# HGRN scores in a hybrid backbone step: who sums the masked levels

## The chip, the core and the metric

The kernel is one program on one core of a Trainium2 chip. The metric is the device time of one execution, in microseconds (us). The engines of the core work side by side, each on its own queue in strict order, and meet only at semaphores: TensorE (PE: matmuls into PSUM; PEld: its weight loads), VectorE (DVE), ScalarE (ACT), GpSimd (POOL) and SyncE (SP, here only issuing DMAs).

## The reference, cut to what matters

Two layers run over 640 tokens (512 latent, 128 context). Each layer has a projection, windowed attention, a gated DeltaNet, HGRN2, an output projection and an FFN (SwiGLU in layer 0, experts in layer 1). The change is in HGRN2. Per direction and head, over chunks of tokens:

```python
b = jnp.cumsum(lf, axis=2)
dec = masked_exp(tri, b[:, :, :, None, :] - b[:, :, None, :, :])
A = jnp.einsum('bhik,bhjk,bhijk->bhij', qc, kc, dec)
o = jnp.einsum('bhik,bhkv->bhiv', qc * jnp.exp(b), S) + A @ vc
S = S * jnp.exp(bl)[..., None] + jnp.einsum('bhck,bhcv->bhkv', kc * jnp.exp(bl[:, :, None] - b), vc)
```

`A` is the matrix of scores: it is zero where the key lies behind the query, and the decay between key and query differs in every one of the 64 channels, so it is no plain matmul.

## The kernel before

The kernel works in chunks of 128 tokens, five per layer (n = 0 to 4, the last one is the context), both directions and four heads at once. A chunk is cut into four **units** x = 0 to 3 (direction and pair of heads); unit u = 4n + x, so 20 units in a layer, and this stage takes about 100 us in each of the two layers.

The decay is split by **levels**: at each of seven powers of two, pairs of blocks share a midpoint, and the decay from key to query is a product of one factor for each side. A matmul of the weighed keys with the weighed queries gives the scores of a level, and a mask keeps the entries that belong to it. Levels that reach no further than 32 tokens, and the diagonal, are the six **near** ones: they are computed as blocks of 32 x 32, masked, and summed. The wider levels need no mask and are copied.

Per unit, with the names of the code:
- `exponents(u)` (PE): four f16 matmuls of 512 columns into slot 0 of PSUM. `decays(u)` (ACT, L1304, L1305) takes the exponential and frees the slot.
- `weigh(u)` (DVE): two products of 128 x 896, the weighed queries and the weighed keys.
- scores (PE, job `A{u}`, slots 2 and 3): 48 small near matmuls and six wide ones. They wait for `weigh(u)`.
- mask (DVE, L2093): 128 x 384 out of PSUM, times `near`, into the buffer `AC[n % 2]`, which holds six levels of 8 x 32 columns. It frees the slot of the scores.
- `wide(u)` (ACT, L1362): three copies of the wide blocks, after the mask.

Per chunk:
- `collect(n)` (DVE, L2055): after the mask of x = 3, three additions (768, 256 and 256 columns) sum the six levels of `AC`.
- `place(n)` (ACT, L1370): four copies of 32 x 256 put the sum on the diagonal blocks of `AH`. It runs on ACT in unit 4(n+1), after `decays(u + 2)`.
- `keys(n + 1)`: PE turns the next chunk's keys and sums its log gates into slot 1 (job `hk`, L2669) in unit 4n; ACT copies them out.
- `carry(n)` (PE, in unit 4(n+1) + 1): the output of the chunk and the update of the state, from `AH`.
- `upper_gates(n + 2)` (ACT, L1278 and L1281): four steps in unit 4n + 2, for n < 3 only.

What sets the order: each engine's list is written out by hand, and `psum_plan` gives each PSUM job one of four slots and a turn in it. `open_(job)` on PE waits until the job before it in the same slot has been freed. PE's order in one unit is exponents(u + 2), scores of u, then for x = 0 `keys(n + 1)`, for x = 1 `carry(n - 1)`. ACT's order is decays(u + 2), for x = 0 `place(n - 1)` and `keys(n + 1)`, `wide(u)`, then for x = 2 `upper_gates(n + 2)`. DVE's is weigh(u + 1), for x = 2 the update of the state, the mask of u, and for x = 3 `collect(n)`. Behind the last unit, PE sums squares (job `rsL`) and starts the output projection (`mixer`), which waits for weights that ACT and POOL (L804) split in two.

Of the kernel before, what the change touches and what calls it, by code (L numbers as in the profile page):

```python
# [15 lines left out]
ALU = mybir.AluOpType  # L16
ACT = mybir.ActivationFunctionType
# [135 lines left out]
def psum_plan():  # L153
# [4 lines left out]
    for l in range(DEPTH):  # L158
# [27 lines left out]
        for u in range(UNITS):  # L186
            n, x = divmod(u, 4)
            j += [f"{2 + u % 2}:A{u}"]
            j += [f"0:E{u + 2}"] if u + 2 < UNITS else []
            j += [f"1:hk{n + 1}"] if x == 0 and n < 4 else []  # L190
            j += [f"1:rs{x - 1}"] if u in (1, 2) else []
            j += [f"1:hs{n - 1}"] if x == 1 and n else []
        j += ["1:rsL", "0:wo0", "1:hs4", "2:wo1", "1:rsC", "3:wo2", "1:wo3", "0:wo4", "2:wo5", "1:wo6", "0:wo7"]
# [70 lines left out]
def backbone_kernel(nc, x_prompt, x_sample, cache_k, cache_v, state_gdn, state_hgrn, c, c_ctx, w_mod, b_mod, w_in,  # L264
# [12 lines left out]
    with ctx:  # L277
# [160 lines left out]
        def mixed(i, k):  # L438
# [56 lines left out]
            "hg_ready lp_hi lp_lo kk_exp kk_ready kw_ready qb_ready qe_ready ke_ready ac_ready ah_ready o_zero o_sq oc_ready oc_sq rs_ready o_ready "  # L495
# [519 lines left out]
        def _(act):  # L1015
# [66 lines left out]
            for l in range(DEPTH):  # L1082
# [282 lines left out]
                def place(n):  # L1365

                    L.need("ac_ready")
                    for b in range(4):
                        r = slice(32 * b, 32 * b + 32)
                        L.do(a.activation(AH[n % 2][r, :, r], AC[n % 2][r, 0], ACT.Copy), "ah_ready" if b == 3 else None)  # L1370
# [286 lines left out]
        def _(dve):  # L1657
# [3 lines left out]
            def tt(o, x, y, op, to=None, job=None):  # L1661
                ins = v_.tensor_tensor(o, x, y, op)  # L1662
                L.free(ins, job) if job else L.do(ins, to)
# [118 lines left out]
            for l in range(DEPTH):  # L1782
# [272 lines left out]
                def collect(n):  # L2055

                    A = AC[n % 2]
                    tt(A[:, 0:3], A[:, 0:3], A[:, 3:6], ALU.add)
                    tt(A[:, 0], A[:, 0], A[:, 1], ALU.add)
                    tt(A[:, 0], A[:, 0], A[:, 2], ALU.add, to="ac_ready")  # L2060

# [12 lines left out]
                for u in range(UNITS):  # L2074
# [14 lines left out]
                    if x == 0 and n >= 2:  # L2089
                        L.need("ah_ready")  # L2090
# [5 lines left out]
                    if x == 3:  # L2096
                        collect(n)
# [5 lines left out]
                L.need("ah_ready", 2)  # L2103
# [144 lines left out]
        def _(pe):  # L2248
# [107 lines left out]
            for l in range(DEPTH):  # L2356
# [381 lines left out]

                def carry(n):

                    L.need("ah_ready")
# [23 lines left out]
                for u in range(UNITS):  # L2765
# [25 lines left out]
                    close(ins, J(f"A{u}"))  # L2791
                    if x == 0 and n < 4:
                        keys(n + 1)
# [7 lines left out]

                L.need("o_sq")
# [265 lines left out]
```

## Time and profile before

| | us |
|---|---|
| median of 3 runs | 2450.79 (2449.39 to 2457.24) |
| the profiled execution | 2452.5 |
| its span, first to last instruction | 2450.7 |
| PE busy | 2143.4 (87%) |
| DVE busy | 1462.0 (60%) |
| ACT busy | 1284.6 (52%) |
| POOL busy | 750.9 (31%) |
| PE's granted clock, mean | 0.94 of full |

The stage of the change lies at about 518 to 622 us (layer 0) and 1591 to 1695 us (layer 1). Busy shares over the whole span say little about it. A matmul's end is modelled and overlaps the next one's start, so how long TensorE holds its queue is better read from the starts of its rows. A granted clock of 1.00 is 2.4 GHz, 0.50 is 1.2 GHz.

### The profile page before, as it was taken

To read this page: it belongs to the slowest core of one execution; us is meant where nothing else is said; L and a number is where in the kernel's file an instruction comes from. 1 tells how busy PE (TensorE), PEld (TensorE's weight loads), DVE (VectorE), ACT (ScalarE), POOL (GpSimd) and SP (SyncE) were. 2 spreads that over 40 slices of the span, in tenths; PEclk is the share of its full clock that TensorE was granted. 3 is DMA by queue.
4 is the path that set the end of the run, shared out by engine and by line. 5 is a ranking of instruction groups with operands and counts; after the bars stand their busy time and mean duration, and the time that the engine had idled before them with its cause. 6 is when DMAs were issued, how large, how long until landed. Compare 5 with 4: busy or idle time off the path is not lost.

```text
span 2450.7 us, 54596 instructions
## 1 busy us (share of the span) xinstructions
PE 2143.4 (87%) x23078; PEld 1334.2 (54%) x23078; DVE 1462.0 (60%) x1822; ACT 1284.6 (52%) x1664; POOL 750.9 (31%) x557
## 2 busy tenths in 40 slices
PE   5998987878989999999898878888969999999990
PEld 3765656755565555555765557654644444444440
DVE  2256735559362121215567665386379999999976
ACT  3443753456534242423533654465268877887862
POOL 0422115332314242423232234333122333333321
PEclk8999987998999999999999888898979999999995
DMA  9222990020212222316220000020276677990023
GB/s 276 98 88 73 309 293 11 3 56 4 72 52 86 69 88 66 103 51 176 81 93 24 1 10 3 3 57 22 92 255 212 224 269 277 329 317 35 27 104 137
DMA packets 215385, 278.46 MB, mean 114 GB/s; under 512 B 28177, under 2 KB 188797, under 8 KB 215039
## 3 DMA queue, kind: packets, MB, share of 16 engines
q1 hardware_dynamic: 203776, 243.60, 30.9%
q0 software_dynamic: 8432, 29.89, 3.3%
q8 instruction: 166, 2.72, 0.5%
q10 hardware_dynamic: 2959, 1.83, 0.3%
q14 instruction: 52, 0.43, 0.1%
HBM read 368.35 MB, written 29.11 MB: 162 GB/s over the span
## 4 chain that ended last, share of the span: by engine, by line
PE 52%; issue 16%; DVE 14%; POOL 8%; ACT 7%; DMA 3%; SPq 1%; POOLq 0%; DVEq 0%; ACTq 0%
PE ps L2268 49%; POOL mix L968 5%; DVE arena L1662 2%; DMA wbuf<-in_w_mod 1%; DVE mix L1670 1%; DVE mix L1662 1%; PE ps L2475 1%; ACT arena L1142 1%; DVE mix L1666 1%; DVE const L1662 1%; DVE yg L1662 1%; DVE hT L1662 1%; DVE xT L1662 1%; POOL mix L971 1%; DVE arena L1666 1%
## 5 line engine op out<-in xcount | busy, mean ns | idle before, releaser
L2268 PE MATMUL ps<-hT,mix 128*128 128x512 f16 (+2 forms) x3024 | 380.0, 288 | 25.1 <-DVE hT L1662 15.2
L2268 PE MATMUL ps<-w,xgT 128*128 128x512 f16 x1632 | 365.4, 381 | 7.3 <-DVE w L2163 7.3
L2268 PEld LDWEIGHTS ps<-hT,mix 128*128 128x128 f16 x3024 | 230.0, 99 | 172.8 <-issue 19.5
L2163 DVE SCALAR_TENSOR_TENSOR w<-wst,w 128x2048 f16<-128x2048 f32 x136 | 310.0, 2320 | 22.7 <-ACT w L1523 22.7
L1000 POOL TENSOR_TENSOR a<-aval,a 128x256 f16<-128x256 f32 x68 | 159.0, 2338 | 371.1 <-ACT a L1571 371.1
L2268 PEld LDWEIGHTS ps<-w,xgT 128*128 128x128 f16 x1632 | 157.4, 98 | 186.0 <-issue 10.5
L1523 ACT ACTIVATE w<-wst 128x2048 f16<-128x2048 f32 x136 | 251.5, 1899 | 6.4 <-DMA xs_rows<-htok,slot_i 6.4
L2268 PE MATMUL ps<-mix 128*128 128x512 f16 (+5 forms) x1856 | 203.5, 286 | 14.5 <-POOL mix L971 8.8
L2268 PE MATMUL ps<-hT,arena 128*128 128x128 f16 (+1 forms) x1440 | 201.2, 301 | 1.1 <-DVE const L1662 1.1
L2268 PE MATMUL ps<-w2m,aT 128*128 128x512 f16 x816 | 188.7, 381 | 5.5 <-DVE aT L2201 5.5
L2268 PEld LDWEIGHTS ps<-mix 128*128 128x128 f16 (+3 forms) x1856 | 120.3, 122 | 88.4 <-POOL mix L971 12.4
L2169 DVE SCALAR_TENSOR_TENSOR w2m<-wst,w2m 128x2048 f16<-128x2048 f32 x68 | 155.8, 2292 | 15.6 <-ACT w2m L1531 15.1
L2127 DVE SCALAR_TENSOR_TENSOR mix<-ps,mix 128x640 f32<-128x640 f32 x22 | 18.1, 825 | 239.3 <-PE ps L2268 239.3
L2268 PEld LDWEIGHTS ps<-hT,arena 128*128 128x128 f16 x1440 | 112.0, 99 | 87.7 <-issue 5.4
L804 POOL TENSOR_TENSOR arena<-wbuf,arena 128x2048 f16<-128x2048 f32 x24 | 100.0, 4165 | 190.7 <-ACT arena L1031 190.6
L968 POOL TENSOR_TENSOR mix<-wbuf,mix 128x2048 f16<-128x2048 f32 x33 | 134.2, 4081 | 57.0 <-ACT mix L1475 57.0
L2268 PEld LDWEIGHTS ps<-w2m,aT 128*128 128x128 f16 x816 | 79.9, 98 | 103.0 <-DVE aT L2201 6.3
L2268 PE MATMUL ps<-arena 64*32 64x32 f32 (+5 forms) x4320 | 103.8, 218 | 31.7 <-issue 17.9
L1531 ACT ACTIVATE w2m<-wst 128x2048 f16<-128x2048 f32 x68 | 129.4, 1903 | 0.2 <-PE ps L2268 0.2
L971 POOL TENSOR_TENSOR mix<-mix 128x640 f16<-128x640 f32 x22 | 30.7, 1395 | 258.2 <-ACT mix L1484 258.2
L2134 DVE TENSOR_TENSOR arena<-arena,ps 128x640 f32<-128x640 f32 x80 | 65.6, 821 | 73.7 <-PE ps L2268 73.7
L2268 PEld LDWEIGHTS ps<-arena 64*32 64x32 f32 (+3 forms) x4320 | 69.9, 115 | 64.2 <-issue 40.5
(360 smaller groups left out, 3604.5 us busy)
## 6 DMA issues: line engine op xcount, KB each, us to landing
wst<-in_moe_w SPq DMA_DIRECT2D x204, 1024.0 KB
wbuf<-in_w_mod SPq DMA_DIRECT2D x40, 1024.0 KB
wbuf<-in_ffn_w SPq DMA_DIRECT2D x33, 1024.0 KB
wbuf<-in_w_in SPq DMA_DIRECT2D x20, 1024.0 KB
xs_rows<-in_table SPq DMA_DIRECT2D x17, 512.0 KB, 6.3
ys_rows<-yb POOLq DMA_DIRECT2D x17, 512.0 KB, 4.0
wbuf<-in_w_out SPq DMA_DIRECT2D x32, 256.0 KB
xg<-xs_rows POOLq DMA_DIRECT2D x16, 512.0 KB, 5.6
```

Of the source, the lines that this page charges most:

```text
L804: L.do(g.tensor_tensor(split_parts(what)[1], wpiece(WP[f"{l}.{what}"][0], n), split_parts(what)[0], ALU.subtract), "w_lo")
L968: g.tensor_tensor(v[1], wpiece(j), v[0], ALU.subtract).then_inc(sg["w_lo"], 1)
L971: g.tensor_tensor(a2[1][:, t], gbuf[:, t], a2[0][:, t], ALU.subtract).then_inc(sg["a_lo"], 1)
L1000: g.tensor_tensor(a16[:, s % 2, 1, :], aval[:, s % 2, :], a16[:, s % 2, 0, :], ALU.subtract).then_inc(sg["m_alo"], 1)
L1523: a.activation(quarter(s, p)[0], staged(s, p), ACT.Copy, scale=WS).then_inc(sg["m_hi13"], 1)
L1531: a.activation(w2p[s % 2][0], staged(s, 2), ACT.Copy, scale=WS).then_inc(sg["m_hi2"], 1)
L1662: ins = v_.tensor_tensor(o, x, y, op)
L1666: ins = v_.tensor_scalar(o, x, s1, s2, op0, op1)
L2134: v_.tensor_tensor(yacc[:, m], yacc[:, m], ps[:, b, 0:NT], ALU.add).then_inc(ps_free[b], 1)
L2163: v_.scalar_tensor_tensor(out=q[1], in0=staged(s, p), scalar=WS, in1=q[0], op0=ALU.mult, op1=ALU.subtract).then_inc(sg["m_lo13"], 1)
L2169: v_.scalar_tensor_tensor(out=q[1], in0=staged(s, 2), scalar=WS, in1=q[0], op0=ALU.mult, op1=ALU.subtract).then_inc(sg["m_lo2"], 1)
L2268: return mm_(o, w, x, start=first, stop=last, skip_group_check=True)
```

## The change

VectorE's three additions per chunk go. In their place PE multiplies each of the six masked levels by the identity matrix and lets PSUM add them up: six f32 products of 128 x 256 in a new job `ac{n}`. ACT's `place` reads the sum from PSUM instead of from `AC`. For n = 0 to 3 the job is put in PE's list right behind the scores of unit 4(n + 1) and ahead of `keys`; for n = 4 it stands behind the last unit, ahead of `rsL`. It takes slot 1 of PSUM, between the jobs that already use that slot: in units 4, 8 and 12 the next job there is `hk` of `keys`. The semaphores `ac_ready` and `ah_ready` go; the slot's own take their place. `AC` is written again only after the job has been filled two chunks before.

```diff
             j += [f"0:E{u + 2}"] if u + 2 < UNITS else []
+            j += [f"1:ac{n - 1}"] if x == 0 and n else []
             j += [f"1:hk{n + 1}"] if x == 0 and n < 4 else []
...
-        j += ["1:rsL", "0:wo0", "1:hs4", "2:wo1", "1:rsC", "3:wo2", "1:wo3", "0:wo4", "2:wo5", "1:wo6", "0:wo7"]
+        j += ["1:ac4", "1:rsL", "0:wo0", "1:hs4", "2:wo1", "1:rsC", "3:wo2", "1:wo3", "0:wo4", "2:wo5", "1:wo6", "0:wo7"]
...
                 def place(n):
 
-                    L.need("ac_ready")
+                    s = L.full(J(f"ac{n}"))[:, 0:256].rearrange("p (m i) -> p m i", m=8)
                     for b in range(4):
                         r = slice(32 * b, 32 * b + 32)
-                        L.do(a.activation(AH[n % 2][r, :, r], AC[n % 2][r, 0], ACT.Copy), "ah_ready" if b == 3 else None)
+                        ins = a.activation(AH[n % 2][r, :, r], s[r], ACT.Copy)
+                        if b < 3:
+                            L.do(ins)
+                    L.free(ins, J(f"ac{n}"))
...
-                def collect(n):
-
-                    A = AC[n % 2]
-                    tt(A[:, 0:3], A[:, 0:3], A[:, 3:6], ALU.add)
-                    tt(A[:, 0], A[:, 0], A[:, 1], ALU.add)
-                    tt(A[:, 0], A[:, 0], A[:, 2], ALU.add, to="ac_ready")
-
...
                     if x == 0 and n >= 2:
-                        L.need("ah_ready")
+                        L.full(J(f"ac{n - 2}"))
...
-                    if x == 3:
-                        collect(n)
...
-                L.need("ah_ready", 2)
                 update(SH, L.full(J("hs4")), ebl[1], J("hs4"), 4, 6)
...
+                def collect(n):
+
+                    L.done(J(f"A{4 * n + 3}"))
+                    s = open_(J(f"ac{n}"))
+                    for v in range(6):
+                        ins = mm(s[:, 0:256], ident, AC[n % 2][:, v].rearrange("p m i -> p (m i)"), v == 0, v == 5)
+                    close(ins, J(f"ac{n}"))
+
                 def carry(n):
 
-                    L.need("ah_ready")
+                    L.done(J(f"ac{n}"))
...
                     close(ins, J(f"A{u}"))
+                    if x == 0 and n:
+                        collect(n - 1)
                     if x == 0 and n < 4:
                         keys(n + 1)
...
+                collect(4)
                 L.need("o_sq")
                 s = open_(J("rsL"))
```

## Rows read from the trace of the kernel before

**Rows 1.** Windows: chunks 1 to 4, then 1 to 3: length; busy PE, PEld, DVE, ACT, POOL; PEclk.
```profile
545.25:565.97 20.72, 15.72 (x508) 9.75 (x505) 19.23 (x26) 15.13 (x35) 5.13 (x8) 0.87 0.01 3
565.97:584.08 18.11, 16.11 (x504) 10.32 (x505) 16.67 (x21) 12.09 (x31) 6.18 (x8) 0.86 0.02 5
584.08:599.89 15.81, 15.39 (x504) 10.08 (x505) 15.23 (x18) 10.41 (x26) 5.75 (x7) 0.89 0.01 3
599.89:615.61 15.72, 11.56 (x489) 8.05 (x490) 11.93 (x18) 8.66 (x21) 3.90 (x4) 0.99 0.02 4
1617.72:1638.72 21.00, 14.37 (x505) 9.34 (x505) 19.70 (x25) 15.12 (x35) 6.18 (x8) 1.00 0.01 4
1638.72:1657.11 18.39, 15.72 (x504) 10.23 (x505) 16.38 (x21) 12.10 (x31) 5.54 (x8) 0.89 0.02 4
1657.11:1673.53 16.42, 15.23 (x504) 9.75 (x505) 15.21 (x18) 10.41 (x26) 6.11 (x7) 0.92 0.02 4
```
**Rows 2.** Chain of waits through layer 1's chunks: start, us, what, instructions.
```profile
1634.19 0.57 DVE mix L1662
...
1638.72 3.08 PE ps L2268 x90
1641.80 1.04 PE ps L2669 x4
...
1644.62 7.16 PE ps L2268 x186
...
1652.59 0.57 DVE mix L1662
...
1657.11 3.43 PE ps L2268 x90
...
1674.24 0.97 DVE mix L1662
```
**Rows 3.** Chain of waits where it runs over VectorE: start, us, what.
```profile
561.44 0.57 DVE mix L1662
...
1617.57 2.07 DVE mix L1662
```
**Rows 4.** Timeline, TensorE's stops inside chunks 1 and 4 of layer 0.
```profile
550.50 1.88 PE L2268 MATMUL ps<-modrow,mix 128*128 128x512 f16 x4 [1.04 <-ACT arena L1305]
602.85 0.25 PE L2268 MATMUL ps<-arena 64*32 64x32 f32 x6 [1.20 <-issue]
```
**Rows 5.** Timeline, VectorE's additions of chunks 0 and 2: start, us, engine, line, tiles, shapes.
```profile
546.00 2.01 DVE L1662 TENSOR_TENSOR mix<-mix 128x768 f32<-128x768 f32 x3
583.92 3.25 DVE L1662 TENSOR_TENSOR mix<-mix 128x768 f32<-128x768 f32 x3
```
**Rows 6.** Timeline, ScalarE: place from SBUF; one step that reads 256 columns of PSUM.
```profile
569.24 1.75 ACT L1370 ACTIVATE mix<-mix 32x256 f32<-32x256 f32 x4
638.39 0.47 ACT L1374 ACTIVATE const<-ps,eps 128x256 f32<-128x256 f32 x1 [5.58 <-PE ps L2268]
```
**Rows 7.** Timeline, TensorE: an f32 product of 256 columns, its successor; exponents.
```profile
637.70 0.59 PE L2268 MATMUL ps<-mix,const 128*128 128x256 f32 x2
638.13 2.10 PE L2268 MATMUL ps<-hT,arena 128*128 128x512 f16 x9
576.98 1.04 PE L2268 MATMUL ps<-modrow,mix 128*128 128x512 f16 x4
```
**Rows 8.** Timeline, TensorE: `keys` in unit 4, layers 0 and 1.
```profile
548.37 0.66 PE L2669 MATMUL ps<-const,extra 128*128 128x128 f32 x4
...
1620.10 0.66 PE L2669 MATMUL ps<-const,extra 128*128 128x128 f32 x4
```
**Rows 9.** Timeline, the end of the stage in layer 0: rsL, weights, mixer.
```profile
615.40 3.66 PE L2268 MATMUL ps<-mix,const 128*128 128x512 f32 x4
617.79 4.21 POOL L804 TENSOR_TENSOR mix<-wbuf,mix 128x2048 f16<-128x2048 f32 x1 [3.56 <-ACT mix L1031]
622.14 4.44 PE L2268 MATMUL ps<-hT,mix 128*128 128x512 f16 x12 [3.08 <-POOL mix L804]
```

More of the change, by code:

```diff
@@ L494, in backbone_kernel @@
             "eg_ready dm_in dm_exp kg_ready egl_ready kd_ready qg_ready cs_ready t_ready t_turned lt_ready "
-            "hg_ready lp_hi lp_lo kk_exp kk_ready kw_ready qb_ready qe_ready ke_ready ac_ready ah_ready o_zero o_sq oc_ready oc_sq rs_ready o_ready "
+            "hg_ready lp_hi lp_lo kk_exp kk_ready kw_ready qb_ready qe_ready ke_ready o_zero o_sq oc_ready oc_sq rs_ready o_ready "
             "near_in wide_ready ltc_ready tt_ready t5_act t6_act ah_clear centred sq_ready rstd_ready scaled xn_ready v_in v_exp "
```

## Prediction

> **What bounds the kernel now.** I read the windows by chunk first, then the chain of waits, then the timeline where the chain changes engine. A window here runs from one `exponents(4n + 2)` to the next. In chunks 1 to 3 VectorE is busy 89 to 96% of the time (15.23 of 15.81 us in chunk 3 of layer 0), TensorE 68 to 97%, ScalarE 63 to 73% [rows 1]. By these shares VectorE is the engine to relieve. The chain tells another story for chunks 2 and 3: from 1638.72 to 1652.5 it stays on TensorE with stops of some tenths only (exponents and scores 3.08, the turned keys 1.04, their log gates and the next exponents, then 7.16 of scores, carry, exponents, scores), crosses VectorE for one mask (0.57), then ScalarE for `wide`, `upper_gates` and `decays`, and is back on TensorE at 1657.11 [rows 2]. VectorE is nearly full there, but beside this ring, not in it. In chunk 1 VectorE leads: the chain enters the additions of chunk 0 at 1617.57 and comes out at the mask of unit 6, at 561.44 and 1634.19 [rows 2, 3]. In chunk 4 VectorE is at 11.9 of 15.7 us, and TensorE has stops of its own, such as 1.20 us in the middle of one unit's scores [rows 1, 4]. So there are two rings, about equally long, and the change takes work from one and puts it into the other.
>
> **What it removes.** The additions took 2.01 us where VectorE was alone and 3.25 beside a GpSimd product [rows 5]. There are ten, but only four are in the chain, two in each layer: 2.0 and 3.3 in layer 0, 3.3 and about 1.9 (it begins at 1674.24 [rows 2]) in layer 1. In all **10.5 us**, the most that their going can give, if nothing else is as late. ScalarE's `place` stays four steps: 1.75 us from SBUF; a step that reads 256 columns of PSUM took 0.47, so 1.9 for four [rows 6]. I keep 1.75.
>
> **What it adds on TensorE.** An f32 product of 256 columns is two instructions. At full clock it takes 0.43 us from the start of its row to the start of the next, and 0.16 more until its end [rows 7]. Six products: 6 x 0.43 = **2.6 us**, at half clock 5.2. They stand in TensorE's strict queue, ahead of `keys`, `exponents` and scores.
>
> **The wait that it adds** is easily overlooked. In units 4, 8 and 12 the next job in slot 1 is `hk`, which `keys` opens right behind `ac`, and it can open only when ScalarE has emptied `ac`. So TensorE stands still for the end of the products (0.16), `place` (1.75) and a semaphore on either side (together 0.1): **2.0 us**. Before, `place` had only `carry` waiting for it, a unit later, and ran beside `keys`. Queued behind the stopped `keys` are `exponents(u + 3)` and the scores of u + 1; for these wait VectorE's mask, then ScalarE's `wide` and `decays`. Together 2.6 + 2.0 = **4.6 us** in each of these units.
>
> **Chunks 2 and 3, both layers** (units 8 and 12). Products and stop fall into the stretch that is TensorE's from end to end, and nothing there waited for the additions. Four times 4.6 is **+18.4 us**. VectorE's relief is worth nothing here: the mask of unit 10 stands in the chain right behind its scores (1652.59 [rows 2]).
>
> **Chunk 1** (unit 4). The scores of unit 4 end where `keys` begins: 548.37 and 1620.10 [rows 8]. Then come 4.6 us of products and stop, then the way from `keys` to the mask two units on. In chunk 2 that way took 10.8 us, 1641.80 to 1652.59, its first part at half clock (`keys` 1.04 there, 0.66 at full [rows 2, 8]). Twice that difference and somewhat more for exponents and scores off it gives 9.4 to 10.3; I take 9.6. The mask of unit 6 comes at 562.6 against 561.44, and at 1634.3 against 1634.19: +1.1 and +0.1, **+1.2 us**. The additions of 2.0 and 3.3 us that leave the chain here are just replaced. TensorE's stop of 1.04 us before `exponents(7)` [rows 4] is swallowed.
>
> **Chunk 4** (unit 16). No `keys` stand behind the products, so there is no stop; `place` runs beside the scores of unit 17. 2.6 us are added in each layer. TensorE's stops in this stretch wait for nothing that the profile shows [rows 4] and look like a supply of instructions that lags behind the short scores; long products give it time. I bound the net between 0 and 2.6 and take half: **+2.6 us** for both layers.
>
> **The tail.** The products of chunk 4 begin 0.8 us after the last scores (mask 0.57 and two waits), and `rsL` comes behind them. Before, TensorE then waited 3.08 us for the weights of `mixer` [rows 9]; layer 1 I take as alike. Against this cover stand 0.8 + 2.6 = 3.4 us at full clock or 6.0 at half. `rsL` itself ran at half clock [rows 9]; put later, it may run at full and give 1.8 back. Bounds per layer -1.5 to +2.9, taken +0.5: **+1.0 us**. The weights move with `carry(3)`, so with the rest. The final `carry(4)` waits for `ac4` behind over 4 us of `mixer`, which hide it.
>
> **Sum.** 18.4 + 1.2 + 2.6 + 1.0 = +23.2 us. On the profiled execution that is 2452.5 + 23.2 = 2475.7; on the median, which is 1.7 lower, **2474 us**.
>
> **The clock** is the largest unknown. Five of the seven windows were granted 0.86 to 0.92 [rows 1], because TensorE is idle for some us before `exponents(10)` and `(14)` and restarts at half: exponents and scores then take 3.08 or 3.43 us [rows 2], and `exponents(7)`, after a stop of only 1.04 us, took 1.88 instead of 1.04 [rows 4, 7]. The new stops of 2.0 us can do the same. If each of the six is followed by a stretch at half clock that costs 1.8 us (0.84 on exponents, about as much on scores), that is +11. If the products run at half in the four chunks that restart so, +2.6 each: +10. If instead the added work keeps the clock up, the four restarts cost some 2 us less each: -8.
> The Trainium skill, "TensorE: Matmul & The Clock Gate", section "What's actually happening", says that the throttled state is the default and activity releases it; by that rule alone more matmuls help the rest, and the sum would be the 8 us lower. The rows bear out the other side of it as well, since even a stop of 1.04 us was followed by half clock once.
>
> **Rivals.**
> *VectorE was the bound, and its relief pays.* If TensorE waits for VectorE longer than 4.6 us in a chunk, products and stop fit into these waits, and the kernel gains what left the chain: 2450.8 - 10.5 = 2440.3. For it: VectorE at 89 to 96%, beside a TensorE that is idle for 5 to 6.6 us in chunk 1 [rows 1]. Against it: in chunks 2 and 3 the idle time is 0.4 to 2.7 us, and what ends it is ScalarE's `decays`. Chance 0.05.
> "Perfetto Trace Analysis" of the Trainium skill, section "Identifying the Most-Contended Engine", says that the most contended engine is the one with the highest occupancy and is to be optimized first; in this stage's windows that is VectorE, and by that rule this rival would be the forecast.
> *The two cancel in part.* VectorE is the later of the rings after all, and hides the stop; then 2.6 us of products count in eight units, and the chain keeps its gain: 20.8 - 10.5, so 2461. Chance 0.12. If more is hidden, no change: 0.03.
> *The stops cost clock as well:* 23.2 + 11, so 2485. Chance 0.18.
> *The product is dearer than I price it.* The weight loads of the identity could show beside the 0.43 us. Bound: 0.2 each (half of the time per instruction pair), 12 x 0.2 x 8 = 19 us, so 2493. In the row of the product they are hidden. Chance 0.04.
> The forecast has the rest, 0.58.
>
> **How the numbers follow.** The range takes in 2461 and 2485: **2459 to 2488**. The forecast's own is 2466 to 2482. A measurement can tell 0.3% from no change, 7.4 us, so 2443.4 to 2458.2 is the same. Faster 0.04, same 0.06, slower 0.90.
>
> **What would show it.** In the profile after: 12 instructions of 128x256 f32 between scores and `keys`, 0.21 us apart; before `keys` about 1.9 us idle on TensorE, ended by ScalarE's `place`, six times; chunks 2 and 3 at about 22.7 and 20.4 us instead of 18.1 and 15.8; chunk 1 unchanged within 1.5 us; VectorE more idle, below 80% in chunks 2 and 3. Wrong would be: `keys` without a wait; chunks 2 and 3 unchanged, which would say that VectorE led them; a granted clock of 1.00 throughout; or products at other than 0.43 us.

## The result and the profile after

The kernel with the change takes 2471.35 us (median of 6 runs, 2467.28 to 2476.63) against 2453.49 us of the kernel before (6 runs beside them, 2449.39 to 2466.86). The ratio is 1.0063, with a 95% interval of 1.0045 to 1.0082, so it is slower by 11 to 20 us, 15.5 in the middle. The medians lie 17.9 apart. The profiled execution took 2473.56 us, span 2471.8.

The span is no good measure for a change of one stage, since stretches outside it move from one execution to the next. So I also read the stage alone: from the start of `decays(0)` to VectorE's first step behind the first part of `mixer`, in both layers. The sum line of these two windows, kernel after (length, busy time of each engine):

```profile
sum 276.06, PE 232.32 PEld 149.56 DVE 168.93 ACT 152.94 POOL 97.19; mean PE 116.16 PEld 74.78 DVE 84.47 ACT 76.47 POOL 48.59
```

The same windows of the kernel before:

```profile
sum 260.50, PE 214.89 PEld 130.61 DVE 190.17 ACT 154.58 POOL 89.80; mean PE 107.44 PEld 65.30 DVE 95.09 ACT 77.29 POOL 44.90
```

VectorE gave up 21.2 us of work, TensorE took on 17.4, and the stage grew by **15.6 us**, as much as the ratio of the runs gives (15.5). Now the windows by chunk, chunks 1 to 4 of layer 0 and the same of layer 1, to lay beside [rows 1]:

```profile
553.38:575.33 21.95, 17.15 (x518) 11.62 (x517) 17.26 (x22) 14.96 (x35) 6.15 (x8) 1.00 0.01 3
575.33:597.32 21.99, 17.95 (x517) 12.08 (x517) 14.22 (x17) 11.94 (x31) 7.22 (x8) 0.92 0.01 4
597.32:616.36 19.04, 16.79 (x516) 11.47 (x517) 13.40 (x15) 10.24 (x26) 7.01 (x7) 1.00 0.01 3
616.36:639.27 22.91, 18.45 (x516) 12.95 (x517) 10.68 (x15) 12.70 (x29) 8.26 (x5) 1.00 0.01 3
...
1633.39:1655.48 22.09, 16.96 (x516) 11.54 (x516) 17.95 (x22) 14.96 (x35) 7.21 (x8) 0.98 0.01 4
1655.48:1678.64 23.16, 19.11 (x517) 12.71 (x517) 14.22 (x17) 11.94 (x31) 7.21 (x8) 0.87 0.01 3
1678.64:1698.79 20.15, 17.90 (x516) 11.82 (x517) 13.34 (x15) 10.25 (x26) 7.03 (x7) 0.92 0.02 4
1698.79:1721.49 22.70, 18.43 (x516) 12.89 (x517) 10.68 (x15) 12.70 (x29) 8.26 (x5) 1.00 0.01 4
```

The fourth window of each layer ends at `mixer`, so it holds chunk 4 and the tail; in the kernel before it was 22.25 and 21.63 us. VectorE is down from 92 and 96% to 65 and 70% in chunks 2 and 3 of layer 0, and these chunks are longer: 21.99 and 19.04 instead of 18.11 and 15.81 us.

TensorE's timeline of the kernel after (start, us, line, tiles, count, and in brackets the idle time before it and what ended it) shows both added parts, in units 8 and 12 of layer 0, then unit 8 of layer 1, and last the tail of layer 0:

```profile
578.50 3.21 PE L2262 MATMUL ps<-mix,const 128*128 128x256 f32 x12
583.55 0.63 PE L2663 MATMUL ps<-const,mix 128*128 128x128 f32 x4 [1.83 <-ACT mix L1371]
...
584.45 1.03 PE L2262 MATMUL ps<-modrow,extra 128*128 128x512 f16 x4
...
599.69 2.86 PE L2262 MATMUL ps<-mix,const 128*128 128x256 f32 x12
604.38 0.63 PE L2663 MATMUL ps<-const,extra 128*128 128x128 f32 x4 [1.83 <-ACT arena L1371]
...
1659.13 3.90 PE L2262 MATMUL ps<-mix,const 128*128 128x256 f32 x12
1664.87 0.63 PE L2663 MATMUL ps<-const,mix 128*128 128x128 f32 x4 [1.83 <-ACT mix L1371]
...
632.79 2.86 PE L2262 MATMUL ps<-mix,const 128*128 128x256 f32 x12 [0.75 <-DVE mix L1666]
637.48 1.96 PE L2262 MATMUL ps<-mix,const 128*128 128x512 f32 x4 [1.83 <-ACT arena L1371]
639.27 2.75 PE L2262 MATMUL ps<-hT,mix 128*128 128x512 f16 x12
```

The twelve instructions, then 1.83 us in which TensorE stands until ScalarE's `place` (L1371) has emptied slot 1, then `keys`: six times alike. From the first product to `keys` it is 4.69 us at full clock and 5.74 in 1659.13, where it began at half. The chain of waits of the kernel after (start, us, what) goes straight through it in chunk 2 of layer 1:

```profile
1655.48 7.56 PE ps L2262 x102
...
1663.13 0.38 ACT mix L1371
...
1664.87 0.63 PE ps L2663 x4
1665.49 8.54 PE ps L2262 x211
```

Against [rows 2] one thing is new: the chain leaves TensorE for `place` between the scores and `keys`.

### The profile page after: what moved, and what is told of

It is laid out like the page before. It is cut to its first block, busy times and chain, and to the rows that moved or that the text cites. A ratio compares the mean times of both kernels' runs of the same rounds, so it can differ in the third digit from the quotient of the medians.

```text
span 2471.8 us, 54816 instructions
## 1 busy us (share of the span) xinstructions
PE 2164.5 (88%) x23198; PEld 1352.4 (55%) x23198; DVE 1440.1 (58%) x1792; ACT 1282.8 (52%) x1664; POOL 758.9 (31%) x557
## 3 DMA queue, kind: packets, MB, share of 16 engines
q10 hardware_dynamic: 2959, 1.83, 0.3%
## 4 chain that ended last, share of the span: by engine, by line
PE 54%; issue 16%; DVE 12%; POOL 7%; ACT 7%; DMA 2%; SPq 1%; POOLq 0%; DVEq 0%; ACTq 0%
PE ps L2262 51%; POOL mix L969 5%; DVE mix L1674 1%; PE ps L2469 1%; DMA wbuf<-in_w_mod 1%; DVE xT L1666 1%; DVE arena L1666 1%; ACT arena L1143 1%; DVE mix L1670 1%; DVE yg L1666 1%; DVE const L1666 1%; DVE arena L1670 1%; POOL mix L972 1%; SPq L701 1%; DVE mix L1803 1%
## 5 line engine op out<-in xcount | busy, mean ns | idle before, releaser
L2262 PE MATMUL ps<-hT,mix 128*128 128x512 f16 (+2 forms) x3024 | 377.3, 288 | 17.9 <-DVE hT L1666 14.8
L2262 PEld LDWEIGHTS ps<-hT,mix 128*128 128x128 f16 x3024 | 229.4, 99 | 163.0 <-DVE hT L1666 11.4
L2262 PE MATMUL ps<-mix,const 128*128 128x256 f32 (+5 forms) x420 | 79.6, 378 | 31.4 <-ACT mix L1449 15.8
```

The costliest lines, as they stand in the source:

```text
L2262: return mm_(o, w, x, start=first, stop=last, skip_group_check=True)
```

## The experiments

The ratio is that of the runs to the kernel before, with its 95% interval; the third column is its excess over 1 times 2453.5 us. The last three come from one profiled execution each, as read above. "From `decays(6)`" is the stage without its beginning, the stretch from `decays(0)` to `decays(6)`, in both layers; "chunks 2, 3" are the distances from `decays(10)` to `decays(14)` to `decays(18)` on ScalarE, layer 0 then layer 1.

| kernel | ratio | us | stage, us | from `decays(6)` | chunks 2, 3 |
|---|---|---|---|---|---|
| before | 1 | 0 | 260.5 | 193.5 | 17.6, 15.9; 19.0, 16.0 |
| after | 1.0063 (1.0045 to 1.0082) | +15.5 | 276.1 | 208.1 | 21.6, 19.5; 23.2, 19.7 |
| e2_stop_only | 1.0050 (1.0030 to 1.0070) | +12.3 | 273.2 | 202.8 | 18.0, 19.0; 20.0, 16.6 |
| e3_products_only | 1.0051 (1.0031 to 1.0072) | +12.5 | 272.3 | 204.9 | 20.1, 18.8; 19.7, 18.7 |
| e4_no_additions | 0.9978 (0.9964 to 0.9991) | -5.4 | 254.0 | 186.7 | 17.6, 15.2; 17.6, 15.8 |
| e1_slot3 | 1.0052 (1.0036 to 1.0069) | +12.8 | 276.9 | 206.7 | 20.5, 19.1; 20.4, 19.1 |
| e8_no_stop | 1.0055 (1.0035 to 1.0076) | +13.5 | 270.5 | 200.1 | 20.3, 19.0; 20.5, 19.1 |
| e5_f16 | 1.0075 (1.0054 to 1.0096) | +18.4 | 282.9 | 215.2 | 23.0, 19.1; 21.6, 21.4 |
| e10_filled_stop | 1.0012 (0.9996 to 1.0028) | +2.9 | 267.3 | 198.5 | 19.5, 18.5; 19.5, 18.4 |
| e9_no_stop_f16 | 0.9984 (0.9969 to 0.9999) | -3.9 | 260.8 | 191.2 | 17.4, 15.8; 20.7, 16.1 |
| e11_filled_before | 1.0015 (0.9996 to 1.0033) | +3.7 | 263.8 | 195.2 | 17.6, 16.2; 17.6, 16.6 |
| e12_filled_no_stop_f16 | 0.9963 (0.9945 to 0.9980) | -9.1 | 254.1 | 183.4 | 17.1, 15.7; 17.1, 15.7 |
| e6_pool | 1.0154 (1.0129 to 1.0179) | +37.8 | 300.0 | 232.4 | 24.3, 22.5; 24.9, 22.0 |

How far to trust a stage of one execution, the unchanged kernel told:

> The kernel before, unchanged, profiled once more: how far one profile's stage length repeats. Stage 260.5 in the first; within 2 us if single profiles can carry comparisons of 5 us and more.

It took 2448.37 us, and its stage 262.3 against 260.5. So a difference of 2 us between two stages says nothing. And that it is no more is luck: the stretch from `decays(0)` to `decays(6)` in layer 1 took 34.10 us the first time and 37.39 the second, the one behind `mixer` 23.88 and 22.53. The first of these matters for all that follows. Every wait, product and filler that the experiments add or take away comes behind `decays(6)`; ahead of it lie only the additions of chunk 0, for which nothing up to `decays(6)` waits, and the masks, which write f16 in some kernels. And yet this stretch took 32.5 to 36.9 us in layer 0 and 31.7 to 37.4 in layer 1 over the 14 profiled executions. In layer 1 the two executions of the unchanged kernel differ there above all in one place: TensorE pauses in the middle of a unit's scores, without a wait that the profile shows, for 1.84 us in the first and 3.96 in the second, and `exponents` behind it took 1.03 and 1.81 us. The column "from `decays(6)`" leaves it out; the unchanged kernel has 193.5 and 191.4 there, so 2 us say nothing in that column either.

### Are both terms real?

The first three kernels start from the kernel before and each do one part of the change alone. Only the stop:

```diff
                     close(ins, J(f"A{u}"))
+                    if x == 0 and 0 < n < 4:
+                        pe.wait_ge(sg["ah_ready"], 5 * l + n)
                     if x == 0 and n < 4:
                         keys(n + 1)
```

> The kernel before, with VectorE's additions and no products, but TensorE waits for place(n) ahead of keys(n + 1) in units 4, 8 and 12. Nothing else changes. Theory: place ended at 570.99 and 589.02 where keys began at 569.60 and 587.17, so 1.4 and 1.9 us are added in chunks 2 and 3, and about 1.5 in chunk 1, where keys would wait until 552.3 but exponents(7) waited until 550.5 anyway: 2 x (1.4 + 1.9 + 1.5) = +9.6 us on 2453.5, 2463. Rival (stops lie beside VectorE's work): within 2 us of 2453.5.

Only the products, written over by the work that follows:

```diff
                     s = open_(J(f"hk{n}"))
+                    if n:
+                        for v in range(6):
+                            mm(s[:, 0:256], ident, am[:, 0:256])
...
                     s = open_(J(f"hs{n}"))
+                    if n == 3:
+                        for v in range(6):
+                            mm(s[:, 768:1024], ident, am[:, 0:256])
...
                 s = open_(J("rsL"))
+                for v in range(6):
+                    mm(s[:, 0:256], ident, am[:, 0:256])
```

> The kernel before, with VectorE's additions and no new wait, plus ten times six f32 products of ident with 256 columns of a constant, written where the next job overwrites them: ahead of keys in units 4, 8 and 12, ahead of carry(3), ahead of rsL. Nobody reads them. Theory: 2.7 us each in full in chunks 2 and 3 of both layers (10.8), nothing in chunk 1, where VectorE leads by more than that, 0.5 to 1.5 in each chunk 4 (2), nothing before rsL, since mixer waits 3.1 and 3.7 us there: +13 us, 2466. Rival (VectorE leads in chunks 2 and 3): under +4 us.

Only VectorE's relief; a step of one element signals in the place of the additions:

```diff
-                    A = AC[n % 2]
-                    tt(A[:, 0:3], A[:, 0:3], A[:, 3:6], ALU.add)
-                    tt(A[:, 0], A[:, 0], A[:, 1], ALU.add)
-                    tt(A[:, 0], A[:, 0], A[:, 2], ALU.add, to="ac_ready")
+                    tt(SB[0:1, 0, 0:1], SB[0:1, 0, 0:1], SB[0:1, 0, 0:1], ALU.add, to="ac_ready")
```

> The kernel before with VectorE's three additions left out and nothing in their place: only one masked level of six is used (one single-element instruction keeps the semaphore). It shows what the relief of VectorE alone is worth. Theory: chunk 1 gains the whole of its additions (2.0 us in layer 0, 3.3 in layer 1), since TensorE's ring is some 3 us shorter there, chunks 2 and 3 nearly nothing, for their ring runs over TensorE: -5.5 us, 2448. Rival (VectorE was the bound of the stage, by its share of busy time): all that left the chain, -10.5 us or more, 2443.

e4_no_additions leaves the sums out, so its output is not the right one; it serves for the time alone. Its gain didn't come where I had expected it: chunk 1 gave 0.7 and 1.0 us, not 2.0 and 3.3, chunks 2 and 3 gave 2.3 together, and the stretch behind `decays(18)` of layer 1 gave 3.0.

The stages moved by +12.7, +11.8 and -6.5 us, the runs by +12.3, +12.5 and -5.4. Of the first, 3.3 us lie ahead of the first stop, in the stretch that moves by itself. From `decays(6)` on it is +9.4, +11.4 and -6.7, together +14.1; the change itself, with all three, made +14.6 there.

The stop alone is no exact copy of the stop in the change, as TensorE's timeline of e2_stop_only shows in units 4 and 8 of layer 0:

```profile
548.18 1.12 PE L2669 MATMUL ps<-const,extra 128*128 128x128 f32 x4 [3.29 <-ACT arena L1370]
...
569.12 0.66 PE L2669 MATMUL ps<-const,mix 128*128 128x128 f32 x4 [1.59 <-ACT mix L1370]
```

Here `place` still waits for VectorE's additions, so the six stops take 3.29, 1.59 and 2.54 us in layer 0 and 4.57, 1.60 and 1.43 in layer 1, 15.0 in all against 11.0 in the change. And some of them cost clock: `keys` behind three of them ran at half clock (1.11 or 1.12 us for 0.66), `exponents` behind four took 1.60 to 1.91 instead of 1.03 (in the kernel before, one of the same six took 1.88). So both parts cost, and the relief gives back a good half of one of them; how the cost divides in the changed kernel itself, this doesn't settle.

### Can the stop be had away?

From the kernel after, the products' job moved to slot 3, behind the scores of unit 4n + 3:

```diff
-            j += [f"1:ac{n - 1}"] if x == 0 and n else []
+            j += [f"3:ac{n - 1}"] if x == 0 and n else []
...
-        j += ["1:ac4", "1:rsL", "0:wo0", "1:hs4", "2:wo1", "1:rsC", "3:wo2", "1:wo3", "0:wo4", "2:wo5", "1:wo6", "0:wo7"]
+        j += ["3:ac4", "1:rsL", "0:wo0", "1:hs4", "2:wo1", "1:rsC", "3:wo2", "1:wo3", "0:wo4", "2:wo5", "1:wo6", "0:wo7"]
...
                     L.done(J(f"A{4 * n + 3}"))
+                    pe.wait_ge(sg["wide_ready"], UNITS * l + 4 * n + 4)
                     s = open_(J(f"ac{n}"))
```

> The changed kernel with one thing different: the job ac lies in slot 3 of PSUM, not in slot 1, so neither keys nor rsL stands behind it; the next user of slot 3 is the scores of unit 4n + 1, which come some 2 us later. Theory (the added stop is part of TensorE's ring and costs its full length where that ring leads): of the eight stops of 1.83 us, the four in chunks 2 and 3 and the two before rsL give it all back, the two in chunk 1 only what that chunk lost (1.1 each): 6 x 1.83 + 2 x 1.1 = 13 us less than the 2471.4 of the changed kernel, about 2458, and the row of keys shows no idle time before it. Rival (the products alone are the price, the stops lie beside VectorE's work): within 2 us of 2471.

Stage 276.9: no gain. In chunks 2 and 3 the stop was gone, as TensorE's timeline shows in the first two lines, with products at 3.87 us because TensorE was at half clock. The last line of it is where I had made two new ones:

```profile
565.62 3.87 PE L2262 MATMUL ps<-mix,const 128*128 128x256 f32 x12
569.33 0.60 PE L2663 MATMUL ps<-const,mix 128*128 128x128 f32 x4
...
622.21 6.28 PE L2262 MATMUL ps<-mix,const 128*128 128x256 f32 x16 [2.96 <-ACT arena L1363]
```

The last products now wait for `wide` (L1363), which in ScalarE's list stood behind two 1.91 us steps for the weights. On VectorE the mask of unit 17 came after 3.30 us of idle time, since its scores in slot 3 waited for `place(3)`:

```profile
611.21 0.56 DVE L1666 TENSOR_TENSOR mix<-ps,nearb 128x384 f32<-128x384 f32 x1 [3.30 <-PE ps L2262]
```

Both were faults of the experiment, so the next kernel takes them out: chunk 3's job stays in slot 1, and chunk 4's products and its `place` come behind `rsL` and its roots.

```diff
-            j += [f"3:ac{n - 1}"] if x == 0 and n else []
+            j += [f"{1 if n == 4 else 3}:ac{n - 1}"] if x == 0 and n else []
...
-                place(4)
                 s = L.full(J("rsL"))
...
                 roots(orsL[1], s[:, LAT:2 * LAT], J("rsL"))
+                place(4)
```

> The changed kernel without any of its stops: ac0 to ac2 in slot 3, where the next user comes two steps later; ac3 in slot 1 as before, where nothing follows for two steps; ac4 in slot 3, its products behind rsL, and place(4) behind the roots on ScalarE. e1_slot3 was meant to do this and moved two of the stops instead (the scores of unit 17 waited for place(3), and the products of chunk 4 waited 2.96 us for a wide copy queued behind the weights on ScalarE). Theory: against the stage of e1_slot3 (276.9 us of both layers, before 260.5) chunk 4 and the tail give back 3.3 us per layer: stage 270, which is +9.5 on before, about 2463 in a median of 2454. What is left is the ten times 2.7 of products less VectorE's relief. Rival (stops are hidden, products are all): stage stays at 276.

Stage 270.5. Against the changed kernel that is 5.6 us less, and 8.0 less from `decays(6)` on, where the stops alone had cost 9.4. The runs give +13.5 with 8.6 to 18.6, which doesn't tell this kernel from the changed one, and the profiled execution was the fastest of its seven. So what the stops cost in the change stands on this one execution.

### What does a product cost, and what does the clock do?

`AC` and the identity in f16, so that each product is one cheap instruction (the masked scores are rounded to f16 before they are summed):

```diff
-        AC = [mem(mix, 3584 + 1536 * i, 6, 8, 32) for i in range(2)]
+        AC = [mix[:, 3584 + 1536 * i:4352 + 1536 * i].bitcast(F16).rearrange("p (v m i) -> p v m i", v=6, m=8) for i in range(2)]
+        identh = states[:, 704:768].bitcast(F16)
...
-                        ins = mm(s[:, 0:256], ident, AC[n % 2][:, v].rearrange("p m i -> p (m i)"), v == 0, v == 5)
+                        ins = mm(s[:, 0:256], identh, AC[n % 2][:, v].rearrange("p m i -> p (m i)"), v == 0, v == 5)
```

> The changed kernel with the masked levels and the identity in f16 instead of f32 (the scores are rounded to f16): a product of 256 columns is then one instruction of 0.11 us, not two of 0.21; slots, waits and stops stay. Theory: the ring over TensorE gets shorter by 6 x 0.43 - 6 x 0.11 = 1.9 us in each of chunks 2 and 3 (7.7), and in chunk 1, which now is TensorE's too, about 1 us each before VectorE leads again; chunk 4 and tail 1 to 2 per layer: -12 us against the stage of the changed kernel (276.1), 264, about 2458. Rival (the stops are all): stage 275.

The opposite happened: 282.9, 6.8 us longer than with the dear products (7.1 from `decays(6)` on). The runs alone (1.0054 to 1.0096 against 1.0045 to 1.0082) don't tell the two apart. TensorE's timeline of this kernel, units 8 and 12 of layer 0:

```profile
575.10 1.46 PE L2264 MATMUL ps<-mix,states 128*128 128x256 f16 x6
578.40 1.09 PE L2665 MATMUL ps<-const,mix 128*128 128x128 f32 x4 [1.84 <-ACT mix L1372]
...
580.13 1.91 PE L2264 MATMUL ps<-modrow,extra 128*128 128x512 f16 x4
...
598.12 0.83 PE L2264 MATMUL ps<-mix,states 128*128 128x256 f16 x6
600.78 0.63 PE L2665 MATMUL ps<-const,extra 128*128 128x128 f32 x4 [1.84 <-ACT arena L1372]
...
601.85 1.91 PE L2264 MATMUL ps<-modrow,mix 128*128 128x512 f16 x4
```

In unit 8 TensorE comes at half clock (1.46 us for the six where full clock takes 0.83), and after the stop of 1.84 us it is still at half: `exponents` take 1.91 instead of 1.03. In unit 12 it comes at full clock, and falls to half within a microsecond after the stop. Behind all six stops of this kernel `exponents` took 1.74 to 1.91 us. With f32 products that never happened: there they took 1.03 in all six places. To see whether it is the idle time that does it, the stop was filled with seven matmuls of 512 columns into a half of the slot that nobody reads:

```diff
                     close(ins, J(f"ac{n}"))
+                    if n < 3:
+                        for i in range(7):
+                            mm(s[:, 512:1024], identh, hg16[:, 0, 0:4])
```

> e5_f16 (the changed kernel with f16 products, stops as they are; stage 282.9 us, 6.8 longer than with the dearer f32 products) plus seven f16 matmuls of 512 columns behind each of ac0, ac1 and ac2, which fill the stop with work that nobody reads (1.5 us at full clock, in the other bank of the slot). Theory (the stop drops TensorE's clock to half when little work surrounds it, and keys, exponents and scores behind it then take up to twice as long): keys behind the stop run in 0.63 again instead of 1.09, and the stage is 7 to 11 us shorter than e5_f16's, 272 to 276, though TensorE does more. Rival (e5_f16 was slow for another reason, such as the f16 writes or chance): the stage stays at 283 or grows by up to 3 x 2 x 1.5 us.

Stage 267.3, which is 15.5 us less, beyond what I had expected, from work that computes nothing. The same place as above:

```profile
566.32 1.67 PE L2264 MATMUL ps<-modrow,states 128*128 128x512 f16 x7
568.32 0.63 PE L2665 MATMUL ps<-const,mix 128*128 128x128 f32 x4 [0.33 <-ACT mix L1372]
...
569.22 1.03 PE L2264 MATMUL ps<-modrow,extra 128*128 128x512 f16 x4
```

`keys` still wait for `place`; most of the idle time has become work, and `exponents` behind the stop take 1.03 us in all six places. So with cheap products the clock cost more than the wait. That the long f32 products do the same for the changed kernel, by keeping TensorE busy around the stop, is the likely reading; the two kernels differ in little else (in this one the masks write f16).

Without stop and with f16 (the two diffs of e8_no_stop and e5_f16 together):

> e8_no_stop and e5_f16 together: no stop, and products of 0.66 us per chunk in place of 2.6 (scores rounded to f16). Theory: both terms of the added 4.6 us are gone but for 0.7 us per chunk, and VectorE's relief stays, worth 6.5 us in the stage by e4_no_additions. Stage 260.5 - 6.5 + 4 x 0.7 + 1 = 258, two or three us under before: 2451 in a median of 2454. Rival (something else in the change costs, such as reading PSUM on ScalarE): stage over 262.

Stage 260.8 and 0.9984: level with the kernel before or just ahead of it. The change's own costs are nearly gone. The clock is not: in layer 0 `exponents(10)` still start at half (1.89 us in place of 1.03), as before the change, and in layer 1 it is `exponents(7)` and `(11)` that took 1.91, the latter in the chunk that took 20.7.

### Which ring leads once the clock is up?

From the kernel before, useless matmuls ahead of `exponents(10)` and `(14)`, to keep TensorE awake in the wait for ScalarE:

```diff
                     d, r = divmod(x, 2)
+                    if u in (8, 12):
+                        s = open_(J(f"hk{n + 1}"))
+                        for i in range(12 if u == 8 else 8):
+                            mm(s[:, 0:512], rev16[:, 0], hg16[:, 0, 0:4])
```

> The kernel before plus idle-time matmuls that nobody reads: 12 of 512 columns in f16 ahead of exponents(10), 8 ahead of exponents(14), where TensorE waits for ScalarE and then restarts at half clock. Nothing is removed. Theory (chunks 2 and 3 are TensorE's ring and half of its clock there is lost to those restarts, some 2 us each): exponents(10) and (14) take 1.04 us instead of 1.3 to 1.9, the stage falls from 260.5 to 252 to 256, about 2447. Rival (VectorE leads there): the stage stays at 260 or more.

The clock did stay up: `exponents(10)` and `(14)` took 1.03 or 1.04 us in both layers, here the first in TensorE's timeline.

```profile
566.53 2.76 PE L2268 MATMUL ps<-modrow,revb 128*128 128x512 f16 x12
570.20 1.04 PE L2268 MATMUL ps<-modrow,extra 128*128 128x512 f16 x4 [0.90 <-ACT arena L1305]
```

Nothing came of it: 263.8, ratio 1.0015, and chunks 2 and 3 of both layers together 68.0 us after 68.5. Its chain of waits in chunk 2 of layer 0 says why:

```profile
570.04 2.07 DVE mix L1662
...
573.33 1.24 DVE arena L1662
...
575.72 0.57 DVE mix L1662
...
583.23 0.57 DVE mix L1662
```

It doesn't touch TensorE at all. Additions (570.04 to 573.31), weighing, mask, weighing, mask: VectorE from end to end, and the same in chunk 3. In layer 1 the chain of the same kernel runs otherwise:

```profile
1640.71 1.07 issue
1641.79 9.10 PE ps L2268 x255
```

It stays on TensorE through chunks 2 and 3, with pauses of 0.7 to 1.1 us that wait for nothing the profile shows, while VectorE, with its additions, stands idle there for 0.50 us at a time. Both chunks are as long as in layer 0 to within 0.5 us. So with the clock up VectorE leads in layer 0, and in layer 1 the two rings are level: where TensorE had led by its half clock, VectorE's ring was right behind it. The same fillers put into e9_no_stop_f16, where the additions are gone as well:

> e9_no_stop_f16 (f16 products, no stops, stage 260.8 us, 2451.8) with the same idle-time matmuls as e11_filled_before. Theory: relief of VectorE and clock add up, since the ring over TensorE gets shorter by the clock and VectorE no longer waits behind its additions: stage 248 to 254, 2442 to 2447, the fastest of all. Rival: VectorE's weigh and mask bound it by then, no better than e11_filled_before.

```profile
564.03 1.03 PE L2264 MATMUL ps<-modrow,extra 128*128 128x512 f16 x4
...
566.40 0.83 PE L2264 MATMUL ps<-mix,states 128*128 128x256 f16 x6
567.06 0.60 PE L2665 MATMUL ps<-const,mix 128*128 128x128 f32 x4
```

Stage 254.1, median 2447.14, ratio 0.9963 (0.9945 to 0.9980): faster than both kernels. Chunk 2 takes 17.1 in both layers, where either measure alone left 17.4 to 20.7 (e9_no_stop_f16) and 17.6 (e11_filled_before). The stage is 6.4 us shorter than that of the kernel before, and 10.1 from `decays(6)` on, well over the 2 us that two executions differ by.

### The additions on GpSimd

The other idle engine. From the kernel before, the three additions go into GpSimd's list after the mask of x = 3, through a wait for the scores' slot:

```diff
+                    if x == 3:
+                        L.done(f"{l}.A{u}")
+                        A = AC[n % 2]
+                        L.do(g.tensor_tensor(A[:, 0:3], A[:, 0:3], A[:, 3:6], ALU.add))
+                        L.do(g.tensor_tensor(A[:, 0], A[:, 0], A[:, 1], ALU.add))
+                        L.do(g.tensor_tensor(A[:, 0], A[:, 0], A[:, 2], ALU.add), "ac_ready")
...
-                    if x == 3:
-                        collect(n)
```

> The kernel before with the three additions per chunk on GpSimd instead of on VectorE or TensorE, at the end of GpSimd's unit 4n + 3; nothing else changes. Theory: TensorE's ring gets nothing added, and VectorE is relieved, so at best the 5.4 us of e4_no_additions. But GpSimd's additions take some 3.3 us per chunk, and where they run together with VectorE's products of two SBUF operands one of them stands still, as the first addition did before (2.1 us beside a GpSimd product, 0.97 alone): of 3.3 us per chunk most comes back on VectorE in chunk 1. Stage between 255 and 261, about 2452. Rival (place and carry wait for the slower additions): stage over 262.

Stage 300.0, the slowest of all. GpSimd's timeline of this kernel first:

```profile
573.63 2.54 POOL L955 TENSOR_TENSOR mix<-mix 128x768 f32<-128x768 f32 x1
576.24 1.46 POOL L956 TENSOR_TENSOR mix<-mix 128x256 f32<-128x256 f32 x1
577.78 1.45 POOL L957 TENSOR_TENSOR mix<-mix 128x256 f32<-128x256 f32 x1
```

VectorE's beside it:

```profile
575.57 1.54 DVE L1668 TENSOR_TENSOR arena<-arena,mix 128x896 f32<-128x896 f32 x1
577.15 1.50 DVE L1668 TENSOR_TENSOR arena<-arena,extra 128x896 f32<-128x896 f32 x1
```

And ScalarE's `place`:

```profile
579.32 1.75 ACT L1376 ACTIVATE mix<-mix 32x256 f32<-32x256 f32 x4 [4.99 <-POOL mix L957]
```

The sum takes 5.45 us, and `place` waits 4.99 us for it on ScalarE, with `wide` and `decays` queued behind. VectorE's products take 1.50 and 1.54 us beside it and 1.09 elsewhere. On these, the Trainium skill, "SBUF — State Buffer", section "SBUF: two separate sides", says that a VectorE step with two inputs from SBUF and a GpSimd step that reads SBUF exclude each other for the whole of an instruction; here each made the other longer. Alone, an addition of 256 columns took 0.72 us (end of layer 1, VectorE idle) and a product 1.09, which is 1.81 one behind the other; side by side such a pair comes every 1.54 us (576.24 to 577.78). That is most of an exclusion, but not the whole of it, going by spans that are rough on GpSimd.

## Why the prediction was right or wrong

The direction and the two costs (products, stop) were right, and the range held the time. The size was 23.2 us against about 15.6. That the time came into the range is in part luck: I had missed two stops, and what was added in chunks 2 and 3 came to 20.2 us instead of 18.4, but the clock, which the sum took as unchanged, gave back more than these. By the terms of the sum, from the windows:

| term | predicted | measured |
|---|---|---|
| chunks 2 and 3, both layers | +18.4 | +3.9, +3.2, +4.8, +3.7 = +15.6 |
| chunk 1 | +1.2 | +1.2, +1.1 = +2.3 |
| chunk 4 and tail | +2.6 and +1.0 | +0.7, +1.1 = +1.7 |
| behind the start of `mixer` | 0 | -1.7, -2.8 = -4.5 |
| up to chunk 1 | 0 | about +0.4 |
| sum | +23.2 | +15.6 |

**The products.** Right: two instructions each, 2.86 us for twelve, of which 2.7 hold the queue (619.03 to 621.72 in chunk 4). Where TensorE came at half clock they took 3.21 and 3.90.

**The stop.** Right in kind, place and size: 1.83 us idle before `keys`, six times, ended by L1371; with the products' end 0.16, it makes 2.0. `place` from PSUM took 1.60 for its four steps, not 1.75; the semaphores took somewhat more than I gave them.

**Chunks 2 and 3** were mis-sized, not in what was added, but in what stayed as it was. From the first product to `keys` the four cases took 5.05, 4.69, 5.74 and 4.69, together 20.2 and so *more* than 18.4. But from the start of `keys` to the next chunk's `exponents` they took 13.77, 11.98, 13.77 and 11.98, where the kernel before had 14.48, 12.72, 15.38 and 13.06: 4.1 us came back. Two steps failed here, the clock and the relief. I took the clock as unchanged in the central case, and it rose: `keys` ran at half before in three of the four places and at full in all of them after (1.60, 1.35 and 1.43 us from their start to `exponents` before, 0.90 after), which is 1.7 us. And I had written that nothing there waited for the additions. In chunk 3 of layer 0 that was false in the trace I had. I had read the chain of waits in layer 1 only; in layer 0 it runs over VectorE there, from the additions of chunk 2 to the mask of unit 14, in the kernel before:

```profile
583.92 2.07 DVE mix L1662
...
587.21 1.24 DVE arena L1662
...
597.17 0.57 DVE mix L1662
```

They are the 3.3 us that I had myself counted among the 10.5 in the chain, and then gave to no chunk. This chunk grew by 3.2 us, the least of the four, with 4.69 added. In all, e4_no_additions puts their going at -2.3 us in these two chunks of both layers (its four legs in the table against those of before). This is near what two executions differ by, but e11_filled_before shows what it means: at full clock the chain in chunk 2 of layer 0 *is* the additions and what stands behind them. I had said myself that the two rings are about equally long, and then priced the relief of one at nothing. The chain of waits names who was last at each point, not by how much.

**Chunk 1** came out 1.1 us dearer over both layers, within the bound of 1.5 each.

**Chunk 4**: no stop behind the products (621.72 follows at once), as said. **The tail** held an error that its own terms hid. I wrote that `rsL` comes behind the products, and didn't follow that it lies in slot 1 too: it can't open until `place(4)` has emptied `ac4`. The timeline shows 1.83 us (the row at 637.48), and in layer 1 it is 1.93. So there are eight stops, not six. They, the products and the late mask were mostly covered by the wait for `mixer`'s weights [rows 9], and `rsL` at full clock (1.96 for 3.66) gave the rest back, which my bounds had contained.

**Behind the tail** I counted nothing, and 4.5 us came back. The first twelve matmuls of `mixer` had taken 4.44 and 5.28 us, after 3.08 and 3.70 idle [rows 9]; now TensorE comes from `rsL` without a stop, and they take 2.75 in both layers, which is 4.2 of the 4.5. In before_again they took 4.76 and 4.19, so by that execution it would be 3.5.

**So most of the 7.6 us is the clock.** It gave 1.7 at `keys` (0.4 of it in chunk 3 of layer 0, where TensorE was not in the chain), 3.5 to 4.2 at `mixer` and 0.4 on the way from `exponents` to the next job, and took 1.4 from the products that began at half: 4 to 5 on balance. The text had this as its bound of -8, at four restarts; the largest share lay at two others, behind the stage. About 2.3 more is the relief that I had priced at nothing, though that is no more than two executions differ by.

**The rivals.** *The stops cost clock as well* was kept off by the products themselves: `exponents` behind all six stops took 1.03 us, and chunks 1 and 3 of layer 0 were granted 1.00 against 0.87 and 0.89 before. It wasn't a wrong fear: with short products (e5_f16) it came true and cost more than they saved, and with none (e2_stop_only) behind four stops of six. With the change's added work the granted clock rose in the three windows of layer 0's chunks 1 to 3, and over chunk 4 with the tail from 0.92 and 0.89 to 1.00; in chunks 1 to 3 of layer 1 it was 0.02 lower twice and the same once. In e5_f16 it was lost around idle time of 1.84 us. The rule cited from "TensorE: Matmul & The Clock Gate" of the Trainium skill, section "What's actually happening", that activity releases the throttle, agrees with the windows that rose, but by itself it would have forecast a rise in layer 1 as well. *The two cancel in part* was the nearest miss: the relief is worth 5.4 to 6.7 us of the 10.5 in the chain (e4_no_additions). *VectorE was the bound*, and with it the rule of occupancy in "Perfetto Trace Analysis" of the Trainium skill, section "Identifying the Most-Contended Engine", fell: VectorE stood at 89 to 96% in these chunks (in chunk 3 of layer 0 TensorE was above it, at 97%), and the kernel that relieves it is 0.6% slower. *A dearer product* fell with 2.86 us for twelve.

What stays open: why TensorE pauses longer in some executions in the stretch ahead of `decays(6)`, and how the cost divides between stop and products in the changed kernel. e2_stop_only and e8_no_stop agree on the stops to within 2 us once that stretch is left out (9.4 and 8.0), but the first has longer stops and loses clock behind them, and the second rests on one execution. In chunk 3 of layer 1, where `keys` had full clock before as well, 0.66 of the 1.1 us that came back were stops of TensorE for which the trace shows no wait.

## What to carry to other kernels

Where two rings are about equally long, work moved from one to the other costs most of its price in the second (15.6 us of 20.2 in chunks 2 and 3). Read the chain of waits in every chunk and layer: it took another way in chunk 3 of layer 0 than in the chunk I read. Price the receiving queue, and ask of each new buffer (a PSUM slot too) who must empty it before the next job in line can open. Before two single executions are compared, look whether they differ in a stretch that the edit can't reach. One measure alone gives next to nothing there (e11_filled_before, e9_no_stop_f16); both together gave 0.4%. And follow the clock through every stretch that starts at half, also behind the stage: it decided the size here, and cheaper matmuls lost it.

## What the runs showed of the hardware

- The granted clock fell around stops of 1.84 us when the work on both sides of them was short (e5_f16: `exponents` behind them 1.74 to 1.91 us), and did not around stops of 1.83 us with 2.86 us of products ahead (after: 1.03). Cheaper products alone made the stage 6.8 us longer, and seven useless matmuls in the stop 15.5 us shorter.
- An f32 product by the identity of 256 columns costs TensorE 0.45 us at full clock (2.69 for six), an f16 one 0.11 (six from 598.12 to their end at 598.95, 0.83 with the last one's way through the array; 0.66 from the first to the start of `keys` in e12_filled_no_stop_f16).
- ScalarE copied 32 x 256 f32 from PSUM in 0.40 us a step (four in 1.60), from SBUF in 0.44 (four in 1.75 [rows 6]).
- On GpSimd an addition of 256 columns took 0.72 us alone and 1.46 beside VectorE, one of 768 took 1.81 and 2.54 (e6_pool); VectorE did all three in 2.0 to 3.3 [rows 5].
